# First block's attention stage: modulations on two PSUM banks in turn, head pairs on four instead of five

## The chip, the cores and the metric

The kernel runs on one core of one Trainium2 chip. The metric is the device time of one execution in microseconds (us); lower is better. PE is TensorE, PEld its weight loads, DVE is VectorE, ACT is ScalarE, POOL is GpSimd, SP is the engine that issues the transfers. `L502` is line 502 of the kernel's file. Names such as `ps` or `w` stand for all buffers of that name.

## The reference

Two transformer blocks run one after the other on 256 tokens of width 1024, all in fp32. The first block holds two attentions and a mixture of experts; the second block holds window attention, latent attention and a neighbourhood attention, and is steered by modulations, which depend on a condition vector alone:

```python
def hybrid_mixer(u, ...):
    y_a = nsa_attention(...) @ w_proj_nsa
    y_b = gla_attention(...) @ w_proj_gla
    mixed = jax.nn.sigmoid(m_a) * y_a + jax.nn.sigmoid(m_b) * y_b
    return mixed @ w_out

def first_block(x, ...):        # x + hybrid_mixer(...), then + hier_moe(...)

def second_block(x, c, ctx, ...):
    mod = silu(c) @ ada_w[layer] + ada_b[layer]      # 1024 x 3072, for each of two layers
    shift, scale, gate = split(mod)
    u = rms_norm_2(h, norm_g[layer]) * (1 + scale) + shift
    ...
```

`nsa_attention` has eight heads of width 64 (three branches each, mixed by gates), `gla_attention` four heads with a decay, and the experts are 32 pairs of matrices of which nearly all weights are read. The modulations need nothing of the first block, so the kernel computes them beside its attention.

## The kernel before

**Order.** Each engine has one instruction stream, written by hand as Python generators, so the order on an engine is fixed when the program is built. Engines meet through semaphores alone. In the attention stage the function `beside` takes one step of the head pairs (`pe_nsa`), then one step of the rest, and `turns` alternates the rest between the modulations (`pe_modulations`) and the decayed attention (`pe_decayed`). ACT, DVE and POOL walk through the same steps with their own parts.

**PSUM banks.** The eight banks `ps0` to `ps7` are handed out by rings. `bank.take(ring, name)` takes the next bank of a ring, and `free` makes PE wait until the bank's last reader is through, whoever that was:

```python
    def next(self):
        b = self.banks[self.at % len(self.banks)]
        self.at += 1
        return b
...
def free(e, t):

    if t.n > 1:
        e.wait_ge(t.evac, t.n - 1)
```

`evacN` counts the reads that empty bank N, `fullN` the groups of matmuls that fill it. Before the change, in this stage, the head pairs have banks 0 to 4 (`FIVE`), the modulations bank 5 alone (`ONE`), the decayed attention banks 6 and 7 (`TWO`). What follows the stage takes its banks from `ALL`, a ring over all eight, which goes on from where it stood earlier in the program.

**Modulations.** There are 12 chunks. For each, PE runs 16 matmuls (two for each of 8 slices, L1004) into a bank, named `ada`; ACT copies it to `rt` (L1026); PE turns `rt` with four transposes (L1015) into a second take, named `ada_sum`; DVE reduces that bank to `mod` (L1042) and adds the bias (L1044). The weights come in 48 loads of 512 KB through ten slots.

**Head pairs.** There are eight pairs (four head pairs by two row tiles), one begun in each step: `scores` takes two banks (L1231), DVE masks them (L1283), ACT takes the exponential (L1327), POOL and DVE weight them (L1337, L1340, L1294). Two steps later `turn` takes two banks for transposes (L1242), ACT copies them (L1314), and `out` takes one bank (L1253, L1260), which DVE copies to `ynT` (L1301). That is five takes for a pair, in a full step in the order turn, turn, scores, scores, out.

**Decayed attention.** Eight levels. At each, POOL makes exponents (L1072, L1073), ACT the exponential (L1097), POOL the scaled queries and keys (L1082, L1083, tiles `la` and `K`), PE two banks of products (L1119), and DVE copies them under a mask (L1158). Its last part (L1131, L559) is read by DVE (L1180), normalised with a root from POOL (L1091), and ends in L1199, counted by `go_done`.

**After the stage.** The last pair calls `project` (L1542) for the first 128 rows of the attention's output projection, half `c = 0`, with the stage's own ring; call its result P0. All later projections take from `ALL`: P1 (the second 128 rows), then the transposes of the decayed attention's output (`ogT`, L570), then the decayed attention's projection of both row tiles, D0 and D1 (L1542 with `kT`), then a gate's projection `m11` (L502). DVE multiplies P0 by its gate (L1894), then D0 by its own (L1898), adds the two (L1900), and does the same for P1 and D1. On DVE's stream L1894 for P0 stands behind the two L1879 of `ogT` and three L496 (the lower halves of `m11`'s weights). Then come the other halves, the mixed output's transposes, and the matmuls with `w_out` (`out0`, `out1`), whose end frees the room for the experts' weights.

`pe_idle` and `pe_idle_next` (L833) are matmuls with no use for the result, put at a few places where PE would wait.

Of the kernel before, what the change touches and what calls it, by code (L numbers as in the profile page):

```python
# [73 lines left out]
class Ring:  # L74
# [3 lines left out]
# [4 lines that stand above are left out]
# [14 lines left out]
# [4 lines that stand above are left out]
# [28 lines left out]
def turns(*works):  # L128

    works = list(works)  # L130
    while works:
        for g in list(works):
            if next(g, works) is works:
                works.remove(g)
            else:
                yield
# [60 lines left out]
def build(nc, d, out):  # L197
    with ExitStack() as ctx:
        sems = {}

        def sem(name):
            if name not in sems:
                sems[name] = ctx.enter_context(nc.semaphore(name))
            return sems[name]
# [6 lines left out]
        bank = Banks(ps, [sem(f"full{i}") for i in range(8)], [sem(f"evac{i}") for i in range(8)])  # L211
# [160 lines left out]
        ynT, ogT = qT, kT  # L372
# [609 lines left out]
        def beside(main, other):  # L982

            for _ in main:
                next(other, None)
            for _ in other:
                pass
# [4 lines left out]
        def pe_modulations(e, ring):  # L992
            for l in range(2):
                for c in range(6):
                    t = bank.take(ring, "ada")
                    free(e, t)
                    if (l, c) == (0, 0):
                        e.wait_ge(cond, 1)
                    for k in range(8):
                        w = W[f"ada{l}{c}.{k // 2}"]  # L1000
                        if k % 2 == 0:
                            e.wait_ge(w.full, w.n)
                        o = slice(32 * (k % 4), 32 * (k % 4) + 32)
                        ins = e.matmul(t.ps[o, :], scT[:, k, :], w.v[:, k % 2, :], start=k < 4, stop=k > 3)  # L1004
                    ins.then_inc(t.full, 1)
                    for m in range(4):
                        W.release(f"ada{l}{c}.{m}", t.full, t.n)
                    yield
                    yield
                    e.wait_ge(t.evac, t.n)  # L1010
                    g = bank.take(ring, "ada_sum")
                    free(e, g)
                    part = rt[:, 2 * (c % 2):2 * (c % 2) + 2, :].rearrange("p a b -> p (a b)")
                    for j in range(4):
                        ins = e.transpose(g.ps[:, j * 128:(j + 1) * 128], part[:, j * 128:(j + 1) * 128], ident)  # L1015
                    ins.then_inc(g.full, 1)
                    yield
                    yield
# [184 lines left out]
        def half(hp):  # L1203
            return slice(64 * hp, 64 * hp + 64)
# [6 lines left out]
        def nsa_steps(work):  # L1211
            for step in range(len(NSA_PAIRS) + NSA_LAG):
                for slot in range(NSA_SLOTS):
                    for at, lag, f in work:
                        if slot == at and 0 <= step - lag < len(NSA_PAIRS):
                            f(step - lag)
                    yield

        def pe_nsa(e, ring, last):
            turned = {}  # L1220

            def scores(p):
                j, i = NSA_PAIRS[p]
                n = 128 * (i + 1)
                ts = [bank.take(ring, "nsa_s") for _ in range(2)]
                for t in ts:
                    free(e, t)
                for kind in range(2):
                    for hp, t in enumerate(ts):
                        o = half(hp)  # L1230
                        ins = e.matmul(t.ps[:, kind * n:kind * n + n], qT[o, j, i * 128:(i + 1) * 128], kT[o, 2 * kind + j // 2, 0:n], start=True, stop=True)  # L1231
                        if kind == 1:
                            ins.then_inc(t.full, 1)

            def turn(p):
                i = NSA_PAIRS[p][1]
                turned[p] = [bank.take(ring, "nsa_t") for _ in range(2)]
                for hp, t in enumerate(turned[p]):
                    free(e, t)
                    e.wait_ge(nsa_norm, 2 * p + hp + 1)  # L1240
                    for c in range(0, 256 * (i + 1), 128):
                        ins = e.transpose(t.ps[:, c:c + 128], NSA_P[(2 * p + hp) % 4][:, c:c + 128], ident)  # L1242
                    ins.then_inc(t.full, 1)

            def out(p):
                j, i = NSA_PAIRS[p]
                t = bank.take(ring, "nsa_o")
                free(e, t)
                if p == 0:
                    e.wait_ge(*emptied("vcd"))  # L1250
                if p < 2:
                    e.wait_ge(*emptied("cmp_t", i))
                e.matmul(t.ps[:, 0:128], vcd[:, j * 128:(j + 1) * 128], cmpT[:, i, :], start=True, stop=False)  # L1253
                for x in turned.pop(p):
                    e.wait_ge(x.evac, x.n)
                for kind in range(2):
                    for k in range(i + 1):
                        c, v = (kind * (i + 1) + k) * 128, 256 + kind * 128 + j // 2 * 64
                        for hp in range(2):
                            ins = e.matmul(t.ps[half(hp), 0:128], kv[:, k, v:v + 64], bT[:, (2 * p + hp) % 3, c:c + 128],  # L1260
                                           start=False, stop=kind == 1 and k == i)
                ins.then_inc(t.full, 1)

            for n in range(2):
                e.wait_ge(*emptied("krT", n))
            def behind(p):
                if p == len(NSA_PAIRS) - 1:
                    last()

            return nsa_steps([(0, 2, turn), (0, 0, scores), (1, 2, behind), (5, 2, out)])  # L1270
# [127 lines left out]
        abs_a, soft_a, roped, pos_used = sem("abs_a"), sem("soft_a"), sem("roped"), sem("pos_used")  # L1398
        c_top, c_exp, c_sum, c_rec, c_norm = (sem(f"cmp_{n}") for n in ("top", "exp", "sum", "rec", "norm"))
        gates, mix_done, cmp_rows = sem("gates"), sem("mix_done"), sem("cmp_rows")  # L1400
        ALL, SIX, FIVE, ONE, TWO, FOUR, MOE = Ring(*range(8)), Ring(0, 1, 2, 3, 4, 5), Ring(0, 1, 2, 3, 4), Ring(5), Ring(6, 7), Ring(0, 1, 2, 3), Ring(4, 5, 6, 7)

        def use(name, i=-1):
            t = bank[name][i]
# [2 lines left out]
        def emptied(name, i=-1):  # L1407
            t = bank[name][i]
            return t.evac, t.n


        def pe_first(e):
# [120 lines left out]
            def project(n, x, p, c, i, first, done, ring=ALL):  # L1533
                ts, t = slice(i * 128, (i + 1) * 128), bank.take(ring, p + str(c))
                free(e, t)
                for y in done:
                    e.wait_ge(y.evac, y.n)
                for k in range(4):
                    w = W[f"{p}{c}.{k // 2}"]
                    if first and k % 2 == 0:  # L1540
                        e.wait_ge(w.full, w.n)
                    ins = e.matmul(t.ps[:, :], x[:, k, ts], w.v[:, k % 2, :], start=k == 0, stop=k == 3)  # L1542
                ins.then_inc(t.full, 1)
                if not first:
                    for k in range(2):
                        W.release(f"{p}{c}.{k}", t.full, t.n)

            decayed = pe_decayed(e, TWO)
            for _ in range(DECAY_AHEAD):
                next(decayed)  # L1550
            rest = turns(pe_modulations(e, ONE), decayed)
            beside(pe_nsa(e, FIVE, lambda: project("nsa_o", ynT, "pnsa", 0, 0, True, bank["nsa_o"][0::2], FIVE)), rest)

            for c in range(2):
                if c == 1:
# [1868 lines left out]
        @block.tensor  # L3424
        def _(e):
            pe_first(e)
            W.ring, W.context = Ring(*range(12)), Ring(*CONTEXT)
            pe_route(e, pe_context_a(e))
            marks.append(len(W.order))
            W.fours = Fours(FOURS, (13, 14, 15, 17, 18, 16))  # L3430
            experts(e, lambda g: pe_sparse(g, pe_context(g)), lambda g: pe_dense(g, pe_context(g)), True)
            marks.append(len(W.order))
            last = W.tiles[[k for k in W.order if k[0] == "few"][-1]].slot
            W.ring, W.last, W.context = Ring(*range(8)), {}, None
            W.ring.at = 4 if last == FOURS[0] else 0
            pe_second(e)
# [179 lines left out]
```

## Time and profile before

| what | value |
|---|---|
| median of 3 runs | 1205.48 us (1204.73 to 1206.25) |
| the profiled execution: its own time | 1208.11 us |
| its span, first to last instruction | 1206.3 us |
| granted TensorE clock, mean over the span | 0.982 |
| PE busy | 1090.4 us (90%) |
| DVE, ACT, POOL busy | 469.1, 412.0, 205.7 us |
| DMA, mean | 277 GB/s |

The span leaves out what lies ahead of the first and behind the last instruction, 1.8 us here. In a line of the timeline the number in brackets is how long the engine sat idle ahead of the group and what released it. A count `x16` means that sixteen instructions were merged. Matmuls overlap each other, so PE's starts tell more than its ends. Clock 1.00 is 2.4 GHz and 0.50 is 1.2 GHz.

### The profile page before, as it was taken

The page shows a single profiled execution, that of the slowest core. Times are in us where ns is not written, and L with a number is a line of the kernel's source. Part 1 is how long each engine was busy: PE and PEld are TensorE (multiplying, and loading weights), DVE is VectorE, ACT ScalarE, POOL GpSimd, SP SyncE. Part 2 cuts the span into 40 slices and gives each one's busy share as a digit, 9 for nine tenths or more (in the row PEclk, how much of TensorE's full clock was granted, in tenths as well). Part 3 has the DMA queues.
Part 4 walks back from the last instruction along what each step waited for, and adds up shares of the span by engine and source line. Part 5 has one row for each costly group of instructions (what it writes and reads, how often), then busy time and mean ns, then how long its engine had stood idle before and what let it go on. Part 6 is the DMA issues. An engine that isn't in the chain of part 4 may idle for free. (4 is left out here: it accounts for less than half of the span.)

```text
span 1206.3 us, 17372 instructions
## 1 busy us (share of the span) xinstructions
PE 1090.4 (90%) x6862; PEld 707.8 (59%) x6862; DVE 469.1 (39%) x1037; ACT 412.0 (34%) x786; POOL 205.7 (17%) x277
## 2 busy tenths in 40 slices
PE   8999888999888889788889799979999899999997
PEld 7886555557432324344444235336887686999775
DVE  4565456445200001123333112106747546454654
ACT  5444443343001001114332102004435454445872
POOL 1005553000000000003120000004522133001550
PEclk9999999998999989999999999999999999999998
DMA  9656499736599999999999999995531213666300
GB/s 366 232 175 255 164 354 317 293 133 268 236 426 425 424 426 417 421 428 400 419 425 420 412 422 418 424 419 198 179 128 53 89 33 115 221 189 187 99 16 35
DMA packets 55720, 333.58 MB, mean 277 GB/s; under 512 B 5840, under 2 KB 6096, under 8 KB 43216
## 3 DMA queue, kind: packets, MB, share of 16 engines
q1 hardware_dynamic: 55632, 332.39, 70.9%
q8 instruction: 57, 0.93, 0.3%
q14 instruction: 31, 0.25, 0.1%
HBM read 331.32 MB, written 1.05 MB: 276 GB/s over the span
## 5 line engine op out<-in xcount | busy, mean ns | idle before, releaser
L486 ACT ACTIVATE ab<-w 128x1024 fp32r<-128x1024 f32 (+2 forms) x117 | 122.1, 1049 | 177.4 <-PE ps L502 168.8
L496 DVE TENSOR_TENSOR ab<-w,ab 128x1024 fp32r<-128x1024 f32 (+2 forms) x96 | 117.3, 1227 | 132.1 <-ACT ab L486 131.8
L2568 PE MATMUL ps<-w,vT 128*32 128x512 f32 x1024 | 125.1, 613 | 41.2 <-DMA w<-in_w_gate 26.9
L502 PE MATMUL ps<-ab,uA 128*128 128x512 f32 x320 | 102.5, 402 | 5.8 <-POOL ab L496 2.7
L2568 PEld LDWEIGHTS ps<-w,vT 128*32 128x32 f32 x1024 | 28.7, 110 | 120.1 <-issue 72.7
L502 PE MATMUL ps<-UA,ab 128*128 128x256 f32 x512 | 93.8, 284 | 2.8 <-ACT h L1584 1.5
L502 PE MATMUL ps<-ab,UA 128*128 128x512 f32 (+1 forms) x288 | 87.8, 386 | 0.2 <-POOL UB L624 0.2
L2616 PE MATMUL ps<-w,bT 128*32 128x512 f32 x512 | 65.1, 634 | 20.0 <-DMA w<-in_w_down 14.5
L502 PEld LDWEIGHTS ps<-UA,ab 128*128 128x128 f32 x512 | 80.2, 192 | 3.5 <-issue 1.7
L496 POOL TENSOR_TENSOR ab<-w,ab 128x1024 fp32r<-128x1024 f32 (+1 forms) x21 | 50.4, 2404 | 132.3 <-DVE Am L1818 88.1
L502 PEld LDWEIGHTS ps<-ab,uA 128*128 128x128 f32 x320 | 60.8, 193 | 20.6 <-issue 3.4
L502 PE MATMUL ps<-UB,ab 128*128 128x256 f32 x256 | 72.4, 283 | 0.0
L2701 DVE TENSOR_TENSOR h<-h,ps 128x512 f32<-128x512 f32 x28 | 19.3, 688 | 116.3 <-PE ps L2593 116.3
L502 PE MATMUL ps<-ab,uB 128*128 128x512 f32 x160 | 63.4, 396 | 0.0
L502 PEld LDWEIGHTS ps<-ab,UA 128*128 128x128 f32 x288 | 53.8, 188 | 10.4 <-POOL UB L624 0.6
L502 PE MATMUL ps<-ab,UB 128*128 128x512 f32 (+1 forms) x144 | 55.4, 385 | 0.0
L2002 PE MATMUL ps<-cst,Uc 128*128 128x512 f32 (+1 forms) x112 | 51.7, 604 | 0.0
L502 PEld LDWEIGHTS ps<-UB,ab 128*128 128x128 f32 x256 | 49.1, 192 | 0.3 <-issue 0.2
L2616 PEld LDWEIGHTS ps<-w,bT 128*32 128x32 f32 x512 | 14.3, 113 | 56.4 <-issue 27.1
L935 ACT ACTIVATE bP<-bS,st 128x512 f32<-128x512 f32 x48 | 34.3, 715 | 23.0 <-DVE st L915 22.0
L2002 PEld LDWEIGHTS ps<-cst,Uc 128*128 128x128 f32 x112 | 20.7, 194 | 31.3 <-issue 27.1
L945 ACT ACTIVATE bT<-ps 128x512 f32<-128x512 f32 x64 | 35.1, 584 | 3.9 <-PE ps L888 3.9
(547 smaller groups left out, 1857.6 us busy)
## 6 DMA issues: line engine op xcount, KB each, us to landing
w<-in_w_gate SPq DMA_DIRECT2D x32, 2048.0 KB, 13.5
w<-in_w_up SPq DMA_DIRECT2D x32, 2048.0 KB, 12.9
w<-in_w_down SPq DMA_DIRECT2D x32, 2048.0 KB, 13.7
w<-in_w_ada SPq DMA_DIRECT2D x48, 512.0 KB, 7.1
w<-in_w_c SPq DMA_DIRECT2D x42, 512.0 KB, 4.5
w<-in_w_m SPq DMA_DIRECT2D x16, 512.0 KB, 5.6
w<-in_ab_out_w SPq DMA_DIRECT2D x10, 512.0 KB, 4.2
w<-in_w_out SPq DMA_DIRECT2D x8, 512.0 KB, 9.8
```

Of the source, the lines that this page charges most:

```text
L486: e.activation(sp.a(j), w.v, ACT.Copy).then_inc(sp.whole, 1)
L496: e.tensor_tensor(sp.b(j), w.v, sp.a(j).bitcast(F32), ALU.subtract).then_inc(sp.parts[j % NAB], 1)
L502: ins = e.matmul(out_, l[x], r[y], start=start and n == 0, stop=stop and n == 2)
L935: ins = e.activation(bP[:, u % 3, :], src, ACT.Exp, bias=m[:, hp:hp + 1], scale=-1.0, accum_out=m[:, 2 + hp:3 + hp])
L945: e.activation(bT[:, u % 3, :], t.ps[:, :], ACT.Copy).then_inc(t.evac, 1)
L2002: ins = e.matmul(t.ps[:, 0:cols], U[:, 2 * c + k, i * 128:(i + 1) * 128], w.v[:, k, 0:cols], start=c + k == 0, stop=c + k == 4)
L2568: ins = e.matmul(t.ps[o, :], ve[:, p % 2, 2 * c + k, o], w.v[:, 2 * a + k, :], start=c + k == 0, stop=c + k == 4)
L2616: ins = e.matmul(t.ps[o, :], hT[:, p % 2, f * 128 + CAP * a:f * 128 + CAP * a + CAP], w.v[:, a, c * 512:c * 512 + 512], start=f == 0, stop ...
L2701: e.tensor_tensor(o, o, t.ps[:, :], ALU.add).then_inc(t.evac, 1)
```

## The change

Two rings are swapped for others. The modulations take banks 4 and 5 in turn, so each `ada` falls on bank 4 and each `ada_sum` on bank 5. The head pairs and P0 take from `FOUR`, banks 0 to 3. `FOUR` is the ring object that the work on the context rows uses later, which therefore begins one bank further on (41 takes, modulo 4). No instruction is added, removed or moved on any engine; only banks and the semaphores waited on differ.

```diff
-        ALL, SIX, FIVE, ONE, TWO, FOUR, MOE = Ring(*range(8)), Ring(0, 1, 2, 3, 4, 5), Ring(0, 1, 2, 3, 4), Ring(5), Ring(6, 7), Ring(0, 1, 2, 3), Ring(4, 5, 6, 7)
+        ALL, SIX, TWO_ADA, TWO, FOUR, MOE = Ring(*range(8)), Ring(0, 1, 2, 3, 4, 5), Ring(4, 5), Ring(6, 7), Ring(0, 1, 2, 3), Ring(4, 5, 6, 7)
...
-            rest = turns(pe_modulations(e, ONE), decayed)
-            beside(pe_nsa(e, FIVE, lambda: project("nsa_o", ynT, "pnsa", 0, 0, True, bank["nsa_o"][0::2], FIVE)), rest)
+            rest = turns(pe_modulations(e, TWO_ADA), decayed)
+            beside(pe_nsa(e, FOUR, lambda: project("nsa_o", ynT, "pnsa", 0, 0, True, bank["nsa_o"][0::2], FOUR)), rest)
```

On PE, early in the stage, around the second chunk's start (L1004) and the first chunk's transposes (L1015); `w9` is the chunk's first weight slot:

```order
 L1119 MATMUL ps<-la,K 128x128 [waits evac7,evac6,scaled]
 L1119 MATMUL ps<-la,K 128x128 x3
-L1015 MATMUL ps<-cst,rt 128x128 [waits evac5]
+L1015 MATMUL ps<-cst,rt 128x128 [waits evac5,evac4]
 L1015 MATMUL ps<-cst,rt 128x128 x3
-L1004 MATMUL ps<-w,scT 32x512 [waits w9,evac5]
+L1004 MATMUL ps<-w,scT 32x512 [waits w9,evac4]
```

Before, a chunk's first matmul waits for bank 5, which DVE's reduction of the chunk ahead empties. After, it waits for bank 4, which ACT's copy of the chunk ahead emptied, and that is what the transposes have waited for already.

On PE, at the end of the stage, before the change: P0, the last pair's `out`, and P1 (numbers of buffers are shown here, so `ps4` is bank 4):

```order
L1542 MATMUL ps4<-w_3,qT 128x512 [waits evac3,evac1,w3,evac4]
L1542 MATMUL ps4<-w_3,qT 128x512
L1542 MATMUL ps4<-w_4,qT 128x512 [waits w4]
L1542 MATMUL ps4<-w_4,qT 128x512
L1253 MATMUL ps0<-yn 128x128 [waits evac0]
L1260 MATMUL ps0<-bT,kv 64x128 [waits evac3,evac2]
L1260 MATMUL ps0<-bT,kv 64x128 x7
L1542 MATMUL ps0<-w_3,qT 128x512 [waits evac3,evac0]
```

And the same place after it:

```order
L1542 MATMUL ps3<-w_3,qT 128x512 [waits evac0,evac2,w3,evac3]
L1542 MATMUL ps3<-w_3,qT 128x512
L1542 MATMUL ps3<-w_4,qT 128x512 [waits w4]
L1542 MATMUL ps3<-w_4,qT 128x512
L1253 MATMUL ps0<-yn 128x128 [waits evac0]
L1260 MATMUL ps0<-bT,kv 64x128 [waits evac2,evac1]
L1260 MATMUL ps0<-bT,kv 64x128 x7
L1542 MATMUL ps0<-w_3,qT 128x512 [waits evac1,evac3,evac0]
```

Behind these rows stand, the same in both kernels, the two groups of `ogT` transposes, then D0 and D1:

```order
L570 MATMUL ps1<-cst,q 128x128 [waits evac1,go_done]
L570 MATMUL ps1<-cst,q 128x128 x3
L570 MATMUL ps2<-cst,q 128x128 [waits evac2]
L570 MATMUL ps2<-cst,q 128x128 x3
L1542 MATMUL ps3<-w_5,kT 128x512 [waits evac2,w5,evac1,evac3]
L1542 MATMUL ps3<-w_5,kT 128x512
L1542 MATMUL ps3<-w_6,kT 128x512 [waits w6]
L1542 MATMUL ps3<-w_6,kT 128x512
L1542 MATMUL ps4<-w_5,kT 128x512 [waits evac4]
L1542 MATMUL ps4<-w_5,kT 128x512
L1542 MATMUL ps4<-w_6,kT 128x512 x2
```

P0 has moved from bank 4 to bank 3; P1 (bank 0), D0 (bank 3) and D1 (bank 4) have stayed. So the next to take P0's bank was D1 before, and is D0 now. The row of D0 reads the same in both, but the count of `evac3` that it waits for now includes DVE's read of P0.

On DVE, the read of P0 (L1894) and what stands ahead of it and behind it:

```order
 L496 TENSOR_TENSOR ab0<-w_8,ab0 128x1024 [waits s1_whole]
 L496 TENSOR_TENSOR ab0<-w_9,ab0 128x1024 [waits s1_whole]
-L1894 TENSOR_TENSOR grow<-ps4,grow 128x512 [waits full4,gates]
+L1894 TENSOR_TENSOR grow<-ps3,grow 128x512 [waits full3,gates]
 L1898 TENSOR_TENSOR bS<-ps3,grow 128x512 [waits full3]
 L1900 TENSOR_TENSOR grow<-grow,bS 128x512 [waits evac3]
```

The read has kept its place, behind the L496, and only its bank has changed.

## Rows read from the trace of the kernel before

**Rows 1.** Stages: us, then busy (count) of PE, PEld, DVE, ACT, POOL; PEclk, DMA share, GB/s

```profile
137.60:220.00 82.40, 70.05 (x639) 41.25 (x639) 42.46 (x161) 40.28 (x109) 35.69 (x77) 1.00 0.87 308
220.00:250.00 30.00, 28.38 (x100) 17.40 (x99) 14.21 (x16) 10.21 (x14) 0.95 (x2) 1.00 0.74 281
370.00:500.00 130.00, 115.84 (x610) 46.46 (x606) 15.72 (x31) 11.37 (x18) 0.62 (x1) 0.96 1.01 423
```

**Rows 2.** Timeline of SP: the first experts' weights behind the stage

```profile
281.01 6.08 SPq L3327 DMA_DIRECT2D w<-in_w_gate  x3
```

**Rows 3.** PE's waits in the stage: us in total, times, longest

```profile
PE ps L1119 <- POOL K L1083: 4.8, 5, 1.6
PE ps L1004 <- DVE mod L1042: 3.7, 5, 1.4
```

**Rows 4.** Timeline of PE in the stage

```profile
142.38 1.92 PE L1004 MATMUL ps<-w,scT 128*32 128x512 f32 x16 [0.35 <-DVE mod L1042]
...
148.24 1.92 PE L1004 MATMUL ps<-w,scT 128*32 128x512 f32 x16 [1.39 <-DVE mod L1042]
...
151.53 1.16 PE L1119 MATMUL ps<-la,K 64*128 64x128 f32 x16
...
172.86 1.92 PE L1004 MATMUL ps<-w,scT 128*32 128x512 f32 x16 [0.54 <-DVE mod L1042]
...
176.31 1.16 PE L1119 MATMUL ps<-la,K 64*128 64x128 f32 x16 [0.52 <-POOL K L1083]
...
178.86 1.13 PE L1231 MATMUL ps<-kT,qT 64*128 64x256 f32 x8
...
206.09 1.92 PE L1004 MATMUL ps<-w,scT 128*32 128x512 f32 x16 [1.09 <-DVE mod L1042]
```

**Rows 5.** Timelines of ACT, POOL and DVE in the stage

```profile
148.20 0.61 ACT L1097 ACTIVATE tmp<-tmp 128x512 f32<-128x512 f32 x1
...
150.27 0.46 POOL L1083 TENSOR_TENSOR K<-qk,tmp 128x128 f32<-128x128 f32 x1
...
175.84 0.29 DVE L1301 COPY qT<-ps 128x128 f32<-128x128 f32 x1 [1.50 <-PE ps L1260]
```

**Rows 6.** Timeline of PE, PEld and DVE behind the stage

```profile
220.93 1.12 PE L570 MATMUL ps<-cst,q 128*128 128x128 f32 x8
...
221.60 1.29 DVE L1879 TENSOR_TENSOR kT<-ps,sml 128x512 f32<-128x512 f32 x2 [4.32 <-PE ps L570]
...
222.81 3.49 DVE L496 TENSOR_TENSOR ab<-w,ab 128x1024 fp32r<-128x1024 f32 x3
...
223.14 7.51 PE L1542 MATMUL ps<-w,kT 128*128 128x512 f32 x16 [1.09 <-DVE kT L1879]
...
226.21 0.68 DVE L1894 TENSOR_TENSOR grow<-ps,grow 128x512 f32<-128x512 f32 x1
...
226.95 0.30 PEld L1542 LDWEIGHTS ps<-w,kT 128*128 128x128 f32 x2 [0.96 <-DVE grow L1894]
...
241.39 7.03 PE L1542 MATMUL ps<-w,qT 128*128 128x512 f32 x16
```

**Rows 7.** Timeline of PE: three of its eight longest idle times

```profile
327.49 1.92 PE L2568 MATMUL ps<-w,vT 128*32 128x512 f32 x16 [3.55 <-DMA w<-in_w_up]
...
350.20 3.33 PE L2616 MATMUL ps<-w,bT 128*32 128x512 f32 x16 [2.83 <-DMA w<-in_w_down]
...
814.60 3.23 PE L2616 MATMUL ps<-w,bT 128*32 128x512 f32 x16 [4.37 <-DMA w<-in_w_down]
```

**Rows 8.** PE alone: us, busy (count), PEclk, DMA share, GB/s

```profile
350.20:353.50 3.30, 3.29 (x17) 0.56 1.04 441
...
292.90:298.60 5.70, 5.70 (x10) 0.51 1.01 431
```

**Rows 9.** Timeline of PE: two like groups of eight

```profile
292.91 5.79 PE L2002 MATMUL ps<-w,Uc 128*128 128x416 f32 x8
298.54 2.96 PE L2002 MATMUL ps<-rt,Uc 128*128 128x416 f32 x8
```

## Prediction

> **What bounds the kernel now.** I read the stages first [rows 1]. In the stage that the change touches (137.6 to 220 us) TensorE is busy for 70.1 of 82.4 us and the transfers for 0.87 of the time; behind it (220 to 250) PE is busy for 28.4 of 30 us. Among the experts (370 to 500) the DMA share is 1.01 at 423 GB/s, so there the transfers set the pace. The experts' first weights are issued at 281.01 [rows 2], when the matmuls with `w_out` have let go of the room that they need. So the order is: PE up to 281, the transfers for the next 540 us, PE again to the end. A delay or a gain of PE ahead of 281 moves the start of the transfers, and nothing behind it has slack to take it up; I count it in full.
>
> Next I read PE's waits in the stage [rows 3]: 3.7 us in five waits for DVE's reduction of a modulation (L1042), and 4.8 us in five waits for POOL's scaled keys (L1083). The first is what the change can remove. The second is the next thing behind it. Then I read the timeline of both [rows 4, 5] and of the stretch behind the stage [rows 6], since a ring's banks are inherited by whoever comes next.
>
> **The change part by part.**
>
> *The modulations' wait goes, 3.7 us at most.* With `ada` on bank 4, a chunk's first matmul waits for ACT's copy of the chunk ahead, which its transposes have waited for anyhow. So the five waits of rows 3 and 4 vanish. What is late next decides how much of that is kept.
> - The first wait (0.35) is kept at once: the second chunk starts at 142.03 instead of 142.38.
> - The second (1.39) lets the third chunk start 1.39 + 0.35 = 1.74 early. But behind it stands L1119, which started at 151.53 and needs K, written by POOL's last L1083 of that level, from 150.27 to 150.73 [rows 4, 5]. This runs behind ACT's L1097 (148.20), which stands in ACT's stream behind the exponentials of pair 1; these follow PE's scores, which come only 0.35 early. So K is there at 150.73 - 0.35 = 150.38, PE starts 0.05 later (about 150.43), and the gain is 151.53 - 150.43 = **1.1 us**; the other 0.65 become a wait for POOL.
> - The two waits in the middle (the 0.54 at 172.86 and one like it, 3.7 - 0.35 - 1.39 - 1.09 - 0.54 = 0.3) are each followed by an L1119 that waits for POOL itself (0.52 at 176.31) [rows 4]. K does not come earlier than the 1.1 already won, since its chain runs L1119, mask copy, DVE's mask of the scores, ACT, POOL. Both count for nothing.
> - The last (1.09, at 206.09) comes when the decayed attention is over on PE. What follows it on PE (copy by ACT, transposes, the last two pairs, P0) hangs on PE's own pace, so it is kept: **1.1 us**.
>
> Sum of this part: -2.2 us. Bounds: -3.7 if no wait comes in place of a removed one, -1.1 if the last is lost to POOL's root or DVE's copies.
>
> *Five banks become four.* In a full step the five takes now move round four banks. A bank of `scores` was emptied a step ago by the mask; now its second bank may instead be the last `out`'s, read by DVE's L1301. The tightest case is pair 5: L1301 runs from 175.84 to 176.13, the scores at 178.86 [rows 4, 5], so it is hidden by 2.7 us. `out` now shares a bank with its own first `turn`, whose copy it needs anyhow. Cost 0; without that cover it would be the 0.29 us of an L1301 at a time.
>
> *P0 moves to bank 3, and D0 is next in bank 3.* This is the part that the diff does not tell, and the one on which the sign rests. D0 now cannot start before DVE has read P0 (L1894). Before, D0 started at 223.14, after DVE's L1879, and L1894 ran from 226.21 to 226.89, behind three L496 that take 3.49 us [rows 6]. It was D1 that waited for it, with its first weights at 226.95, and the trace names L1894 as the releaser. So D0 takes over this time: it starts at about 226.98 instead of 223.14, 3.84 late. D1 then follows with no wait. D0 and D1 took 7.51 with the stop between them, while a like run of sixteen (at 241.39) took 7.03; 0.08 of the difference is the longer first matmul after a stop (it took 0.67, the usual one 0.59), which stays, so about 0.40 comes back. Cost: 3.84 - 0.40 = **+3.4 us**. Nothing else is queued on PE that could run in the gap: `m11` (L502) and everything up to `out1` stand behind D0. L1894 itself is not delayed, since all that it waits for (L1879, the ACT halves of `m11`'s weights) stands ahead of D0, and it moves with the -2.2. Bounds: +3.0 if the restart costs a bit less, +3.9 if nothing comes back.
>
> *The clock after the gap.* PE ends the `ogT` transposes at 222.05 and then idles to 226.98: 4.9 us, with 1.1 us of transposes ahead of it. The trace has eight idle times of 2.8 to 4.4 us on PE. After three, sixteen 32-column matmuls took their usual 1.92 us (the one after 3.55 us is shown); after five they were slower, such as 3.33 after 2.83 us and 3.23 after 4.37 [rows 7], with a granted clock of 0.56 from 350.2 to 353.5, which is mostly the 1.2 GHz level [rows 8]. The new gap is longer than all of these, so I take a drop as likelier than none. Price: 3.33 - 1.92 = 1.4 us. Where PE stays dense a longer drop costs more: eight L2002 took 5.79 at clock 0.51 and 2.96 when it was back [rows 8, 9], 2.8 us. I take **+1.4**, with 0 and +2.8 as ends. The Trainium skill (TensorE: Matmul & The Clock Gate, section Why this matters for your kernels) asks for no long idle of PE between bursts of matmuls, since the clock falls back after one; the trace agrees in five cases of eight. The same page (section Loop structure matters more than you think) shows a copy out of PSUM by DVE between matmuls as harmless to the clock; by that the sum would be 1.4 us less, a rival below.
>
> *The ring `FOUR` later.* The context rows' work begins one bank on. Its first takes are banks 1 and 2 instead of 0 and 1, all emptied long before among the `w_out` matmuls; from there on the order repeats. Cost 0.
>
> Sum: -2.2 + 3.4 + 1.4 = **+2.6**. Against the profiled execution, its span 1206.3 becomes 1208.9, and its own time 1208.1 becomes 1210.7. That execution lay 2.6 above the median of the runs shown (1205.48); the change put on the median gives **1208.1 us**.
>
> **The rivals.**
> - *The gap without the drop.* The clock stays up, as after the 3.55 us. -2.2 + 3.4 = +1.2: 1206.7. Against it: the gap is longer than any in the trace.
> - *A longer drop.* -2.2 + 3.4 + 2.8 = +4.0: 1209.5. For it: the one after 292.9 lasted that long.
> - *Only the gain.* D0 finds its bank free after all, or DVE reads P0 sooner. Then -2.2: 1203.3; with all five waits kept, -3.7: 1201.8. This is the other side: it decides by whether L1894 ends before D0's other needs are met (223.1), and three L496 of 1.2 us stand in its way. The Trainium skill (Perfetto Trace Analysis, section Matmuls) says that independent groups of matmuls should rotate through different banks, so that the copy out of one overlaps the next. By that rule the modulations gain and this rival wins; the rule says nothing of who inherits the banks.
> - *Less gain.* POOL or ACT paces the whole stage and only 1.1 is won: with the drop -1.1 + 3.4 + 1.4 = +3.7, 1209.2.
>
> **How the numbers follow.** Chances: the forecast (gap and drop) 0.50, the gap without a drop 0.22, a longer drop 0.10, less gain 0.10, only the gain 0.08. The range for 8 in 10 reaches from 1206.3 (no drop, a bit more gain) to 1210.0 (the longer drop and some loss of gain); the forecast's own is 1207.2 to 1209.1. A measurement of this kernel can tell about 0.2%, 2.4 us, from no change. The forecast's +2.6 lies just above that: I put 0.6 of its chance over the line and 0.4 under it. Slower: 0.30 + 0.10 (the longer drop) + 0.10 (less gain) = 0.50. Faster: 0.04, the half of the gain-only case that lies beyond -2.4. Within: the rest, 0.46.
>
> **What the profile after would show.** No wait of L1004 for `mod`; more waits of L1119 for K, 1.1 us won by the third level and 2.2 by the stage's end (the `ogT` transposes at about 218.7 instead of 220.93). Then D0 started by L1894, at about 224.8, after an idle of nearly 5 us, and D1 right behind it. PE at the lower clock there or not decides between forecast and first rival. The first experts' weights issued at 283.6 (forecast) or 282.2. The prediction is wrong if D0 starts before L1894 ends, if the gain in the stage isn't near 2.2, or if the shift at 281 doesn't arrive at the end.

## The result, and the profile after

| | before | changed |
|---|---|---|
| median of 19 runs each | 1207.95 us | 1211.15 us |
| ratio, with its 95% interval | | 1.0034 (1.0023 to 1.0046) |
| profiled execution, its own time | 1208.11 us | 1210.61 us |
| its span | 1206.3 us | 1208.8 us |
| granted TensorE clock, mean | 0.982 | 0.980 |

The change makes the kernel slower by 0.34%, about 4.1 us of 1208. The two medians lie 3.2 us apart (0.26%), which is inside the interval too. One of the changed kernel's 19 runs took 2751.89 us; it is left out of the ratio.

PE's waits of the changed kernel in the stage, to be laid beside [rows 3] (us in total, times, longest):

```profile
PE ps L1119 <- POOL K L1083: 6.3, 6, 1.6
PE ps L1015 <- ACT rt L1026: 2.5, 5, 0.7
```

The wait of L1004 for DVE's reduction is gone, and PE's wait for POOL has grown from 4.8 to 6.3. PE's timeline of the changed kernel shows the stage's ends (the first scores, L1231, and the `ogT` transposes, L570), D0 and D1, and the second group of L1542 with `qT`, to be laid beside [rows 6] (a group at the edge of the window that was read shows only its part inside, here 7 of 16):

```profile
139.62 0.71 PE L1231 MATMUL ps<-kT,qT 64*128 64x128 f32 x8
...
220.79 1.12 PE L570 MATMUL ps<-cst,q 128*128 128x128 f32 x8
226.81 9.77 PE L1542 MATMUL ps<-w,kT 128*128 128x512 f32 x16 [4.90 <-DVE grow L1894]
...
247.34 3.17 PE L1542 MATMUL ps<-w,qT 128*128 128x512 f32 x7
```

From the first scores to the transposes it is 220.79 - 139.62 = 81.17 us; before it was 220.93 - 137.58 = 83.35. So the stage is 2.18 us shorter. Then D0 starts 6.02 us behind the transposes, where it was 2.21, and D0 with D1 takes 9.77 us, where it was 7.51. From the transposes to the second group of `qT` it is 26.55 us against 20.46: 6.09 more. The stretch as a whole loses 6.09 - 2.18 = 3.91 us.

Why D0 and D1 take so long stands in the weight loads' timeline of the changed kernel:

```profile
226.81 0.50 PEld L1542 LDWEIGHTS ps<-w,kT 128*128 128x128 f32 x2 [5.09 <-DVE grow L1894]
227.83 0.34 PEld L1542 LDWEIGHTS ps<-w,kT 128*128 128x128 f32 x1 [0.52 <-issue]
...
231.24 0.34 PEld L1542 LDWEIGHTS ps<-w,kT 128*128 128x128 f32 x1 [0.52 <-issue]
232.09 0.22 PEld L1542 LDWEIGHTS ps<-w,kT 128*128 128x128 f32 x1 [0.52 <-issue]
232.55 0.19 PEld L1542 LDWEIGHTS ps<-w,kT 128*128 128x128 f32 x1 [0.24 <-issue]
232.98 0.19 PEld L1542 LDWEIGHTS ps<-w,kT 128*128 128x128 f32 x1 [0.24 <-issue]
```

The loads of one half follow each other every 0.85 us up to 232.09, and every 0.43 us from then on. The windows of the same stretches (us, then busy time and count of PE, PEld, DVE, ACT, POOL, then the granted clock, the DMA share and GB/s) put the clock at 1.2 GHz and then at 2.4 GHz:

```profile
228.68:231.90 3.22, 3.22 (x5) 1.35 (x4) 0.00 (x0) 0.00 (x0) 0.00 (x0) 0.50 1.03 443
232.98:235.90 2.92, 2.92 (x8) 1.33 (x7) 1.98 (x3) 0.00 (x0) 0.00 (x0) 1.00 0.97 381
```

The last place is SP's timeline, which answers to [rows 2]:

```profile
286.55 0.82 SPq L3327 DMA_DIRECT2D w<-in_w_gate  x2
```

The first experts' weights go out at 286.55, 5.54 us later than the 281.01 of before. Of these 3.91 come from the stretch above, and 2.04 were there before the stage began (first scores at 139.62 against 137.58); 0.41 is given back behind it, mostly in a pause of 0.4 of the context norm (L570) that had stood there. I don't lay the 2.04 to the change. Of the fourteen profiled runs of this study, six have the first scores between 137.5 and 137.9 us, seven between 139.2 and 139.9 and one at 141.03, and one and the same kernel falls on either side (P0 in bank 7, below: 137.61 and 139.36). The changed kernel itself was late in both of its profiles (139.62 and 141.03), but with ten idle matmuls added behind the stage (below) it was early in both (137.87 and 137.53).

### The profile page after: what moved, and what is told of

Read it like the earlier page. It is cut to its first block and busy times, and to the rows that moved or that the text cites. A ratio compares the mean times of both kernels' runs of the same rounds, so it can differ in the third digit from the quotient of the medians.

```text
span 1208.8 us, 17372 instructions
## 1 busy us (share of the span) xinstructions
PE 1094.1 (91%) x6862; PEld 709.2 (59%) x6862; DVE 467.7 (39%) x1037; ACT 412.0 (34%) x786; POOL 205.2 (17%) x277
## 5 line engine op out<-in xcount | busy, mean ns | idle before, releaser
L496 DVE TENSOR_TENSOR ab<-w,ab 128x1024 fp32r<-128x1024 f32 (+2 forms) x96 | 117.8, 1233 | 131.5 <-ACT ab L486 131.4
L496 POOL TENSOR_TENSOR ab<-w,ab 128x1024 fp32r<-128x1024 f32 (+1 forms) x21 | 50.0, 2383 | 133.9 <-DVE Am L1818 88.1
```

The costliest lines, as they stand in the source:

```text
L496: e.tensor_tensor(sp.b(j), w.v, sp.a(j).bitcast(F32), ALU.subtract).then_inc(sp.parts[j % NAB], 1)
```

## The experiments

**Where P0 lies.** The first four kernels ask whether the loss comes from P0's bank. The changed kernel with P0 alone moved back to bank 4, and, as a second kernel, to bank 7:

```diff
-  project("nsa_o", ynT, "pnsa", 0, 0, True, bank["nsa_o"][0::2], FOUR)
+  project("nsa_o", ynT, "pnsa", 0, 0, True, bank["nsa_o"][0::2], Ring(4))   # or Ring(7)
```

> The change as it is, but P0 takes bank 4, as before. My theory (the loss is only that D0 inherits P0's bank, with the clock drop behind the gap; the stage itself gains): the stage from the first scores to the ogT transposes stays at about 81.2 us (83.35 before), D0 starts about 2.2 us behind the transposes, no clock drop there, and the whole is about 2.2 us faster than before, ratio 0.998. Rival 1 (the head pairs on four banks, or the context work one bank on, cost the time): still about 4 us slower than before, ratio 1.003. Rival 2 (no gain in the stage reaches the end): ratio 1.000.

> The change, but P0 takes bank 7, which nobody wants until the projections of c = 1. My theory: as with P0 on bank 4, and D1's small wait for L1894 goes too (about 0.4 us), so 2.6 us faster than before, ratio 0.9978. Rivals as there: 1.003 or 1.000.

Bank 4: 0.9961 of the kernel before (0.9941 to 0.9981). Bank 7: 0.9991 (0.9973 to 1.0008). PE's timeline with P0 in bank 4:

```profile
137.82 0.71 PE L1231 MATMUL ps<-kT,qT 64*128 64x128 f32 x8
...
219.05 1.12 PE L570 MATMUL ps<-cst,q 128*128 128x128 f32 x8
221.26 7.51 PE L1542 MATMUL ps<-w,kT 128*128 128x512 f32 x16 [1.09 <-DVE kT L1879]
...
239.51 7.03 PE L1542 MATMUL ps<-w,qT 128*128 128x512 f32 x16
```

The stage keeps its gain (219.05 - 137.82 = 81.23 us), and behind it everything is as it was before: D0 2.21 us behind the transposes, 20.46 us to the second group of `qT`. With bank 7 D1 is free of the wait too:

```profile
220.97 7.11 PE L1542 MATMUL ps<-w,kT 128*128 128x512 f32 x16 [1.09 <-DVE kT L1879]
```

D0 and D1 take 7.11, which is the 0.40 that the prediction wanted back.

**The wait alone.** The kernel before, with D0 and D1 swapped in their banks, so that D0 stands behind P0 in bank 4 while nothing of the modulations is changed:

```diff
-  project(n, x, p, c, i, i == 0, done)
+  swapped = c == 0 and n == "ogT"
+  project(n, x, p, c, i, i == 0, done, Ring(4 - i) if swapped else ALL)
+  if swapped:
+      ALL.next()
```

> The kernel before, with no ring of the stage touched; only D0 and D1 have swapped banks, so that D0 takes bank 4 behind P0 and D1 takes bank 3. My theory: D0 waits for L1894, an idle of about 4.9 us, the lower clock behind it, and 3.4 us (clock kept) to 6.1 us (clock down as in the changed kernel) slower than before, ratio 1.003 to 1.005; the stage stays at 83.35 us. Rival 1 (four banks or the context work cost the time): no difference, ratio 1.000.

1.0042 (1.0024 to 1.006). In this kernel L1894 has become L1897 (the window shows fifteen matmuls of the group; all sixteen take 8.83 us):

```profile
222.95 1.12 PE L570 MATMUL ps<-cst,q 128*128 128x128 f32 x8
228.97 8.40 PE L1542 MATMUL ps<-w,kT 128*128 128x512 f32 x15 [4.90 <-DVE grow L1897]
```

The idle time is the same 4.90 us, the stage is as long as before (222.95 - 139.56 = 83.39), and from the transposes to the second group of `qT` it is 248.56 - 222.95 = 25.61 us, 5.15 more than before. Two results that trade banks cost 0.42%.

**Filling the gap.** The changed kernel, with matmuls of no use put in the gap, on bank 4:

```diff
+  if (c, n, i) == (0, "ogT", 0):
+      pe_idle(e, Use(ps[4], None, None, 0), 20, LEV)
   project(n, x, p, c, i, i == 0, done)
```

> The change, with 20 matmuls of 128x256 into the free bank 4 ahead of D0 (their results are not used), about 4.7 us at 0.23 each. It parts the gap from the clock. My theory: D0 starts at the same place (6.0 us behind the transposes, released by L1894), but at full clock, D0 and D1 take about 7.0 us instead of 9.8, so 2.7 us faster than the changed kernel and 1.2 us slower than before, ratio 1.001. Rival (the clock falls whatever runs there, or the slow sixteen matmuls have another cause): as the changed kernel, ratio 1.0034.

1.0037 (1.0019 to 1.0054). The twenty are too many; PE's timeline:

```profile
222.02 8.80 PE L833 MATMUL ps<-cst 128*128 128x256 f32 x40
230.66 6.60 PE L1542 MATMUL ps<-w,kT 128*128 128x512 f32 x15
```

An fp32 filler stands in the trace as two matmuls and takes 8.80 / 20 = 0.44 us. They reach four microseconds past the end of L1894: D0 starts 230.66 - 221.07 = 9.59 us behind the transposes and not at the 6.0 expected, so this run tells nothing of the sum; it does show that D0 starts at full speed behind them. I halved them in a second kernel.

> The changed kernel with ten idle matmuls (128x256, about 0.44 us each, so 4.4 us) put into bank 4 of PSUM ahead of D0; they add work whose result nobody reads. They fill the gap that the twenty of the earlier run overran. Theory (the changed kernel pays the wait of D0 and, behind it, TensorE's lower clock): D0 still starts about 6.0 us behind the ogT transposes, released by L1894, but D0 and D1 take 7.0 to 7.6 us in place of 9.77; from the ogT transposes to the second L1542 group of qT about 24 us (26.55 in the changed kernel); ratio to before about 1.001. Rival (the lower clock costs nothing that is not hidden later): ratio as the changed kernel's, 1.0034.

0.9997 (0.9979 to 1.0014). PE's timeline with ten:

```profile
219.03 1.12 PE L570 MATMUL ps<-cst,q 128*128 128x128 f32 x8
219.98 4.48 PE L833 MATMUL ps<-cst 128*128 128x256 f32 x20
225.04 7.13 PE L1542 MATMUL ps<-w,kT 128*128 128x512 f32 x16 [0.58 <-DVE grow L1896]
...
242.93 7.03 PE L1542 MATMUL ps<-w,qT 128*128 128x512 f32 x16
```

D0 still starts 6.01 us behind the transposes, as in the changed kernel (6.02), but D0 and D1 take 7.13 instead of 9.77. So the 26.55 us fall to 242.93 - 219.03 = 23.90. This splits the 6.09 us of the changed kernel's profile: **3.44 for the wait (23.90 - 20.46), and 2.65 for the lower clock.** In the swapped kernel, by the same count, the clock took 25.61 - 23.90 = 1.71.

**Taking the wait away on DVE.** The changed kernel, same banks, with the read of P0 ahead of the `ogT` copies and the three L496:

```diff
+  t = bank["pnsa0"][0]
+  e.wait_ge(gates, 1)
+  e.wait_ge(t.full, t.n)
+  e.tensor_tensor(grow[:, 0, 0:512], t.ps[:, :], grows[:, 0, 0, :], ALU.mult).then_inc(t.evac, 1)
   for i in range(2):
       t = bank["ogT"][i]
...
-  e.wait_ge(t.full, t.n)
-  e.tensor_tensor(o, t.ps[:, :], sm[:, i, 0, :], ALU.mult).then_inc(t.evac, 1)
+  if c + i > 0:
+      e.wait_ge(t.full, t.n)
+      e.tensor_tensor(o, t.ps[:, :], sm[:, i, 0, :], ALU.mult).then_inc(t.evac, 1)
```

> The changed kernel with one edit on VectorE: the read of P0 (L1894 for block half 0) stands ahead of the two copies of the ogT transposes and of the three splits of m11.2, so that bank 3 is free before D0 wants it. Same banks, same number of instructions. Theory (the loss is the wait of D0 on that read): stage about 81.2 us, D0 2.0 to 2.8 us behind the transposes, D0 and D1 at full clock in 7.0 to 7.6 us, about 20.5 to 21 us from the transposes to the second L1542 group of qT; ratio to before 0.996 to 0.999, as P0 in bank 4 gave. Rival (the ring's turn or the four banks cost something of their own): ratio 1.001 or more.

0.9974 (0.9955 to 0.9993). DVE's timeline, where the early read is L1879 and the `ogT` copies are L1883:

```profile
217.02 0.68 DVE L1879 TENSOR_TENSOR grow<-ps,grow 128x512 f32<-128x512 f32 x1
221.43 1.29 DVE L1883 TENSOR_TENSOR kT<-ps,sml 128x512 f32<-128x512 f32 x2 [3.73 <-PE ps L570]
222.63 3.48 DVE L496 TENSOR_TENSOR ab<-w,ab 128x1024 fp32r<-128x1024 f32 x3
```

and PE's:

```profile
139.75 0.71 PE L1231 MATMUL ps<-kT,qT 64*128 64x128 f32 x8
...
220.76 1.12 PE L570 MATMUL ps<-cst,q 128*128 128x128 f32 x8
222.97 7.11 PE L1542 MATMUL ps<-w,kT 128*128 128x512 f32 x16 [1.09 <-DVE kT L1883]
...
240.82 7.03 PE L1542 MATMUL ps<-w,qT 128*128 128x512 f32 x16
```

The read fits into a time in which DVE waited for PE anyway. The stage is 81.01 us, and 20.06 us lie between the transposes and the second group of `qT`. The changed kernel's banks lose nothing once the read is in time.

**Four banks for the pairs, alone.** The kernel before, pairs on banks 0 to 3, P0 in 4, modulations still on 5:

```diff
-  beside(pe_nsa(e, FIVE, lambda: project(..., FIVE)), rest)
+  beside(pe_nsa(e, Ring(0, 1, 2, 3), lambda: project(..., Ring(4))), rest)
```

> The kernel before with its head pairs on banks 0 to 3 alone, P0 held in bank 4 as it is there before, and the modulations still on bank 5 alone. Theory (the fifth bank of the pairs carried nothing): stage 83.3 to 83.6 us, waits of L1004 for VectorE's L1042 as before, ratio 0.999 to 1.001. Rival (the loss of the fifth bank costs): stage 84 us or more, ratio 1.001 to 1.003.

0.9995 (0.9972 to 1.0019). The waits in the stage are those of before to the tenth (3.7, 4.8 and, for L1015, 2.9). The stage itself took 84.95 us, 1.35 more than I had allowed. That is also past the 84 us which the rival had named. The windows show a lower clock, and the waits for banks haven't changed:

```profile
152.16:162.16 10.00, 7.62 (x78) 4.92 (x76) 4.51 (x19) 3.90 (x13) 6.04 (x14) 0.97 1.02 402
162.16:172.16 10.00, 9.44 (x78) 4.55 (x76) 4.06 (x17) 4.18 (x12) 2.43 (x7) 0.86 0.88 297
```

In the profiled run the granted clock fell for a while in the stage (0.86 in the second window); in the profile of the kernel before it is 1.00 over the stage [rows 1], and so it is in the eleven other profiled runs whose head pairs have four banks. What lowered it in this one run stays open.

**The ring's turn.** P0 in bank 4, and the context rows' ring turned by one, as in the changed kernel:

```diff
+  FOUR.next()
   for c in range(2):
       if c == 1:
           pe_lin(e, S1, "m11", uA, uB, 512, range(2))
```

> The changed kernel with P0 in bank 4, as in the run before with ratio 0.996, and with the ring of four turned by one place more behind the stage, as P0 turned it in the changed kernel; it is the ring that the context stream beside the experts goes on with. Theory (the turn costs nothing): ratio 0.994 to 0.998, the same as without it. Rival (the turn makes context matmuls wait for a bank, and is a part of the loss): ratio 0.999 or more.

0.9971 (0.9953 to 0.9989), where the unturned one gave 0.9961. The turn costs nothing that shows.

**Once more, on one chip.** The changed kernel, P0 in bank 4, P0 in bank 7 and the ten fillers again.

> The changed kernel as it stands, once more, on the same chip as the three beside it. Expected 1.0034 of the kernel before again (1.002 to 1.005), from ogT transposes to the second L1542 group of qT 26.5 us.

> The changed kernel with P0 in bank 4, once more: in the first run its ratio was 0.9961, P0 in bank 7 gave 0.9991 and P0 in bank 4 with the ring turned 0.9971, though the three traces agree within 0.4 us from the stage to the first experts' weights. Theory (they are one case, and the rest is scatter of the experts' stage, where the DMA engines are busy all the time): all of them at 0.996 to 0.999 when put together, worth 1.7 to 2.2 us of stage. Rival (bank 4 has a gain of its own behind the stage): this one again under 0.997 while bank 7 stays at 0.999 or more.

> The changed kernel with P0 in bank 7, once more, beside P0 in bank 4. Theory: the same as bank 4 within the intervals, 0.996 to 0.999. Rival: 0.999 or more, over 0.2% behind bank 4.

> The changed kernel with ten idle matmuls ahead of D0, once more, now on the same chip as the changed kernel: the first run gave 0.9997, 0.0037 under the changed kernel's ratio of another job, where the trace shows 2.65 us (0.0022). Theory: 0.001 to 0.004 under the changed kernel of this job. Rival: no difference between the two.

| kernel | ratio to before | 95% interval | first time |
|---|---|---|---|
| changed kernel | 1.0026 | 1.0007 to 1.0044 | 1.0034 |
| P0 in bank 4 | 0.9968 | 0.9956 to 0.998 | 0.9961 |
| P0 in bank 7 | 0.9982 | 0.9962 to 1.0002 | 0.9991 |
| ten fillers | 1.001 | 0.9992 to 1.0029 | 0.9997 |

The fillers lie 0.0016 under the changed kernel, inside the 0.001 to 0.004 expected, but the two intervals overlap: the times alone don't part the clock from the wait, the traces do.

The fillers gave 23.90 us from the transposes to the second group of `qT` again, to the hundredth. The changed kernel shows the same idle time again:

```profile
228.22 8.83 PE L1542 MATMUL ps<-w,kT 128*128 128x512 f32 x16 [4.90 <-DVE grow L1894]
```

but this time the clock was back after 3.5 us (loads every 0.85 us up to 231.74), where in the first profile it took 5.3:

```profile
230.89 0.34 PEld L1542 LDWEIGHTS ps<-w,kT 128*128 128x128 f32 x1 [0.52 <-issue]
231.74 0.19 PEld L1542 LDWEIGHTS ps<-w,kT 128*128 128x128 f32 x1 [0.51 <-issue]
232.17 0.19 PEld L1542 LDWEIGHTS ps<-w,kT 128*128 128x128 f32 x1 [0.24 <-issue]
```

From the transposes (222.21) to the second group of `qT` (247.82) it is 25.61 us, as in the swapped kernel. So the clock's price is 1.71 or 2.65 us, by how long it stays down.

The changed kernel, the fillers and the two kernels with P0 elsewhere come in the order of their traces. Two things stay open. Bank 7 lay 0.0030 and 0.0014 above bank 4, while its traces are no worse: 20.06 us from the transposes to the second group of `qT` against 20.46, and the first experts' weights at 279.19 and 280.10 against 279.54 and 278.62. And bank 4 gains 0.32 to 0.39% (3.9 to 4.7 us of 1208), where the stage shows 2.1 to 2.2. The intervals are about 0.002 wide to either side or less, so neither is settled, and I had no experiment on either.

## Why the prediction was off, point by point

The direction was right and the mechanism was the one forecast. The forecast time, 1208.1 us, missed the measured 1211.15, which lies 1.15 above the range's end of 1210.0. Two terms were mis-sized. The base, 1205.48 from three runs, was 2.47 us too low, and the range held nothing for its scatter; with the base right the same range would have reached to 1212.5 and held the result. The clock drop, +1.4, measured 1.71 to 2.65; with that alone right the forecast would still have been only 1208.4 to 1209.3. The stage's gain (2.18) and D0's wait (3.44) came as summed; that the whole shift reaches the end isn't shown.

- **The stage's gain, -2.2.** Measured 2.18. In the changed kernel nothing of L1004 waits for `mod`; POOL's waits took over 6.3 - 4.8 = 1.5 us. That the sum comes out to 0.02 is partly luck, since its two halves missed in opposite ways. Counted from the first scores, the L1119 of [rows 4] at 151.53 starts 13.95 us on before, and this one 12.63 us on after:

```profile
152.25 1.16 PE L1119 MATMUL ps<-la,K 64*128 64x128 f32 x16 [0.44 <-POOL K L1083]
```

  So 1.32 was won there (forecast 1.1), and by the last modulation but one it was 1.37 (L1004 at 200.39 before and 201.06 after). From there to the transposes only 0.8 came on top (forecast 1.1).
- **Four banks for the pairs, 0.** The kernel with that edit alone has the same waits, and its 0.9995 (0.9972 to 1.0019) shows no cost.
- **D0's wait, +3.4.** D0 starts 6.02 - 2.21 = 3.81 later behind the transposes (forecast 3.84), with L1894 as the releaser and 4.90 us idle (forecast 4.9). The net price, taken with the clock held up by the fillers, is 3.44. That this wait, with the clock drop that follows it, is the cause is shown from three sides: P0 in another bank removes the loss, an earlier read removes it, and the kernel before acquires it by swapping D0 and D1.
- **The clock after the gap, +1.4: too small.** The drop came, and it cost 2.65 us in one profile and 1.71 in the other (and 1.71 in the swapped kernel). I had weighed two prices, 1.4 behind a gap among the experts and 2.8 where PE stays dense [rows 7 to 9], and took the lower as the likelier. Both were read from too little. The 1.4 is what one group of sixteen short matmuls lost; a drop can reach into the group behind it, as these lines of the kernel before show:

```profile
353.46 3.70 PE L2002 MATMUL ps<-cst,Uc 128*128 128x512 f32 x8
...
430.25 2.38 PE L2568 MATMUL ps<-w,vT 128*32 128x512 f32 x16 [2.91 <-DMA w<-in_w_gate]
432.56 4.90 PE L2002 MATMUL ps<-cst,Uc 128*128 128x512 f32 x8
```

  Behind the 2.83 us gap the next group ran at its usual 3.70. Behind the 2.91 us gap the first group lost 2.38 - 1.92 = 0.46 and the next one 4.90 - 3.70 = 1.20 (granted clock 0.50 from 432.60 to 434.90), together 1.66. The 2.8 stands behind no gap at all: PE came to 292.91 without an idle time. What sets the price, as far as these traces tell, is how long the clock stays down while PE has work: a load takes 0.85 us instead of 0.43, so half of that time is lost, 2.65 of 5.3 us and 1.71 of 3.5. Why it stayed down for 5.3 us once and for 3.5 in two other profiles, behind the same idle time, stays open. The stretch gives -2.18 + 3.44 + 1.71 = +2.97 or, with 2.65, +3.91; the latter is my rival of the longer drop (+4.0), to which I had given 0.10. The Trainium skill (TensorE: Matmul & The Clock Gate, section Loop structure matters more than you think) shows DVE's copy out of PSUM as not breaking PE's warmth, with the next matmuls following immediately. Here they could not follow: D0 needed the bank of P0, whose read stood behind other work in DVE's stream, and after the 4.90 us of waiting the granted clock was 0.50 (228.68 to 231.90).
- **The base, the step that put the result outside the range.** I put +2.6 on the median of three runs, 1205.48. The same kernel's median of 19 is 1207.95, so 2.47 of the miss is the base. With that base my own sum gives 1210.6, 0.6 from the measured median. Three runs within 1.5 us of each other had looked tighter than they were: the 19 reach from 1204.73 to 1212.3. The three held a warning: the profiled execution, 1208.11, lay 2.6 above their median, and I noted it without widening the range.
- **That the shift arrives in full: not shown.** The local +2.97 to +3.91 fits the measured 1.0034 (2.8 to 5.6 us of 1208) and 1.0026 (0.8 to 5.3). The profiled spans differ by only 2.5, though the first weights went out 5.54 later. In single executions this proves little: from that issue to the span's end it took 925.3 us before and 922.3 after, and 918.1 to 925.9 in the other profiled runs, with no order by kernel. So the profiled execution's own time, 1210.61 where I forecast 1210.7, agrees by luck: its first weights went out at 286.55 and not at 283.6.
- **The ring turned by one, 0.** The run with it and the one without agree within their intervals.
- **The chances.** Slower had 0.50, no visible difference 0.46. The two sat on one line at +2.4, because the clock's price was taken low.

**What beats both kernels.** The two-bank modulations are good; only P0's place was not. With P0 in bank 4 the kernel runs at 0.9968 (0.9956 to 0.998) of the time before, and with an early read of P0 at 0.9974 (0.9955 to 0.9993).

## What to carry to other kernels

- When a set of buffers shrinks, look at who inherits its last one. A ring that is handed over in the middle of its turn gives the next consumer a bank whose reader may be far back in another engine's stream. Print the bank numbers at the border, not inside the stage alone.
- Price a clock drop by how long the clock stays down behind the gap, over all groups that follow and not the first alone. With dense matmuls half of that time was lost (2.65 of 5.3 us, 1.71 of 3.5). Ten useless matmuls in the gap took that price away and left the wait itself.
- Take the base from many runs, or let the range carry its scatter: the median of three lay 2.47 us under that of 19, against an effect of 3.2 to 4.1.
- The cheapest cure was one read moved into a time when its engine waited anyway (217.02, where DVE would have idled until 221.43).

## What the runs showed that was not expected

- The time ahead of the stage differs by 2 us from run to run, and one wait has to do with it. PE waits near 105 us for POOL's split (L496). This timeline is the changed kernel's:

```profile
105.59 1.03 PE L502 MATMUL ps<-ab,uA 128*128 128x512 f32 x2 [3.96 <-POOL ab L496]
106.42 0.63 PE L502 MATMUL ps<-ab,uB 128*128 128x512 f32 x1
...
109.80 0.40 PE L502 MATMUL ps<-ab,uB 128*128 128x512 f32 x1
```

  In the changed kernel PE came to it early (the group ahead starts at 97.97, before at 98.88), waited 3.96 us instead of 2.68, and then ran at 0.63 a matmul instead of 0.40 until about 109. The five profiled runs with a wait of 3.9 us or more there all reached the stage late (139.56 or later); of the nine with 2.8 or less, six came early and three late. What delays those three stays open. A difference of 2 us between two traces means nothing if it arises there.
- The same idle time of 4.90 us, ahead of the same matmuls, kept the clock at 1.2 GHz for 5.3 us in one profiled run of the changed kernel and for 3.5 us in the other. The price of a gap is not one number, even in one kernel.
